# The gate table's one-hot matrices: the unscaled ones in one VectorE comparison, the scaled ones spread over three engines

## What is computed

```python
PEER_HEADS, PEER_NKEYS, PEER_TOPK = 8, 128, 16
...
best_s, best_pos = lax.top_k(cand_s.reshape(c, PEER_HEADS, -1), PEER_TOPK)
idx = jnp.take_along_axis(cand_i.reshape(c, PEER_HEADS, -1), best_pos, axis=-1)
gate = jax.nn.softmax(best_s, axis=-1)
ue = u[idx]
ve = v[idx]
act = jax.nn.gelu(jnp.einsum('td,thkd->thk', xc, ue).astype(jnp.float32), approximate=False)
return jnp.einsum('thk,thkd->td', (gate * act).astype(xc.dtype), ve)
```

## Time and profile before

| what | value |
|---|---|
| time, median of three runs | 3128.49 us |
| profiled execution, span from first to last instruction | 3124.2 us |
| what lies around the span, by the median | 4.3 us |
| PE busy | 3004.4 us, 96% |
| PEld busy | 2520.8 us, 81% |
| DVE busy | 2348.2 us, 75% |
| ACT busy | 1530.3 us, 49% |
| POOL busy | 297.5 us, 10% |
| gate stage, first layer | 1324.6 to about 1429 us |
| gate stage, second layer | 2410.3 to about 2516 us |

### The profile page before, as it was taken

The page is one execution under the profiler, slowest core; times in us unless marked ns, Lnnn a source line. Parts: engine busy times, 40 slices in busy tenths (PEclk is TensorE's granted clock), DMA queues, the critical chain, the costliest instruction groups (busy, mean ns, idle before and its releaser), DMA issues.

```text
span 3124.2 us, 51394 instructions
## 1 busy us (share of the span) xinstructions
PE 3004.4 (96%) x16392; PEld 2520.8 (81%) x16392; DVE 2348.2 (75%) x5143; ACT 1530.3 (49%) x2678; POOL 297.5 (10%) x412
## 2 busy tenths in 40 slices
PE   7999999989998999999999999999999999999998
PEld 4888887769887879877888888778798778888887
DVE  5777787556656866997777777777679977777776
ACT  3222223345754655196555554446552955555544
POOL 0000000000000005092000000000051910000000
PEclk9999999999999999999999999999999999999999
DMA  7333332223222334413555555523343135555553
GB/s 273 105 120 107 116 107 109 88 78 135 82 103 100 106 138 149 148 35 138 187 187 187 186 187 197 188 95 121 122 162 135 41 135 188 188 188 187 187 190 134
DMA packets 75386, 439.74 MB, mean 141 GB/s; under 512 B 7233, under 2 KB 8769, under 8 KB 34433
## 3 DMA queue, kind: packets, MB, share of 16 engines
q1 hardware_dynamic: 72592, 419.15, 37.8%
q0 software_dynamic: 2528, 18.02, 1.6%
q10 hardware_dynamic: 144, 0.98, 0.1%
HBM read 437.08 MB, written 1.05 MB: 140 GB/s over the span
## 4 chain that ended last, share of the span: by engine, by line
PE 84%; DVE 8%; ACT 2%; DVEq 2%; issue 2%; ACTq 0%; DMA 0%; POOL 0%; SPq 0%
PE bank L471 17%; PE bank L473 17%; PE bank L472 17%; PE bank L2341 10%; PE bank L2343 5%; PE bank L2272 4%; DVE arena L2543 2%; PE bank L1512 2%; PE bank L879 1%; PE bank L868 1%; PE bank L1229 1%; PE bank L1247 1%; PE bank L558 1%; DVE arena L1564 1%; DVEq L2543 1%
## 5 line engine op out<-in xcount | busy, mean ns | idle before, releaser
L450 ACT ACTIVATE peer_r<-wring 128x512 fp32r<-128x512 f32 x1328 | 826.5, 631 | 807.9 <-PE bank L473 538.0
L455 DVE TENSOR_TENSOR peer_r<-wring,peer_r 128x512 fp32r<-128x512 f32 x1264 | 857.5, 692 | 393.3 <-ACT peer_r L450 390.1
L2341 PE MATMUL bank<-res_r,peer_r 128*128 128x512 f32 x1344 | 479.9, 397 | 3.4 <-DVE peer_r L455 3.4
L471 PE MATMUL bank<-h_r,peer_r 128*128 128x512 f32 (+1 forms) x1088 | 397.5, 365 | 22.1 <-DVE h_r L666 15.4
L471 PE MATMUL bank<-peer_r 128*128 128x512 f32 x1024 | 404.5, 395 | 2.8 <-DVE peer_r L2574 2.8
L473 PE MATMUL bank<-peer_r 128*128 128x512 f32 x1024 | 401.3, 392 | 0.0
L472 PE MATMUL bank<-peer_r 128*128 128x512 f32 x1024 | 399.6, 390 | 0.0
L473 PE MATMUL bank<-h_r,peer_r 128*128 128x512 f32 (+1 forms) x1088 | 385.2, 354 | 0.0
L2343 PE MATMUL bank<-res_r,peer_r 128*128 128x256 f32 x1344 | 376.9, 280 | 0.0
L472 PE MATMUL bank<-h_r,peer_r 128*128 128x512 f32 (+1 forms) x960 | 334.9, 349 | 0.0
L2341 PEld LDWEIGHTS bank<-res_r,peer_r 128*128 128x128 f32 x1344 | 252.5, 188 | 64.2 <-DVE peer_r L455 4.0
(11 more groups left out here) (392 smaller groups left out, 5033.5 us busy)
## 6 DMA issues: line engine op xcount, KB each, us to landing
wring<-in_w_peer SPq DMA_DIRECT2D x256, 1024.0 KB, 4.8
wring<-in_w_proj SPq DMA_DIRECT2D x34, 1024.0 KB, 4.8
wring<-in_w_hy SPq DMA_DIRECT2D x32, 1024.0 KB, 5.3
arena<-in_w_ada POOLq DMA_DIRECT2D x16, 1024.0 KB, 5.1
wring<-in_w_out SPq DMA_DIRECT2D x16, 1024.0 KB, 4.8
wring<-in_w_ada SPq DMA_DIRECT2D x8, 1024.0 KB, 11.1
wring<-in_w_hyout SPq DMA_DIRECT2D x8, 1024.0 KB, 4.9
wring<-in_w_q SPq DMA_DIRECT2D x8, 1024.0 KB, 4.8
```

The costliest lines, as they stand in the source:

```text
L450: act.activation(SPLIT[:, buf, 0, :], raw_quarter(name, i, j, q), ACT.Copy).then_inc(split_hi, 1)
L455: v.tensor_tensor(SPLIT[:, buf, 1, :], raw_quarter(name, i, j, q), SPLIT[:, buf, 0, :].bitcast(F32), ALU.subtract).then_inc(split_lo, 1)
L471: pe.matmul(out_ap, w_hi, x_hi, start=start, stop=False, **kw)
L2341: pe.matmul(two_parts(acc[:, :]), SPLIT[:, buf, 0, w], h_both[:, k, :, :], start=(k == 0), stop=False, skip_group_check=True)
```

## The change

The unscaled one-hots of a group are now all made by VectorE, by one `tensor_tensor` comparison of 128 x 512 (the column numbers, repeated four times, against the four tokens' column, each repeated 128 times). The scaled ones are shared: GpSimd makes those of tokens 2 and 3 by `tensor_scalar` with two operations, in every group. Token 1's is made by ScalarE in three groups of four: NEAR = |iota - i|, then relu(g - g NEAR), where g is the gate weight. VectorE makes token 0's, and in the fourth case (n a multiple of 4) token 1's as well. ScalarE needs the negated gate weights for this, and two more activations ahead of the stage write them to a new array, `NEGG`. TensorE waits for `hot_c` only in the groups where ScalarE contributes.

```diff
@@
+        NEGG = wide_t[:, 2 * P:2 * P + T]
@@
                 pe.wait_ge(hot, x + 1)
                 pe.wait_ge(hot_b, x + 1)
-                pe.wait_ge(hot_c, x + 1)
+                if b:
+                    pe.wait_ge(hot_c, 3 * (x // 4) + b)
@@
             a.then_inc(pair_ready, 1)
+            for tt in range(2):
+                act.activation(NEGG[:, tt * P:(tt + 1) * P], bank[2 + tt][:, 0:P], ACT.Copy, scale=-1.0)
             act.drain()
 
             def hots_scalar(n):
 
                 act.wait_ge(g_done, GROUPS * l + n + 1)
-                t = 4 * (n % 2) + 1
-                act.activation(NEAR[:, n % 2, :], iota, ACT.Abs, scale=-1.0, bias=pair[:, 2, n // 2, t, :])
+                t, near = 4 * n + 1, NEAR[:, n % 2, :]
+                act.activation(near, iota, ACT.Abs, scale=-1.0, bias=PAIR[:, 1, t:t + 1])
                 act.drain()
-                act.activation(OHB[:, t, :], NEAR[:, n % 2, :], ACT.Relu, scale=-1.0, bias=ones[:, 0:1]).then_inc(hot_c, 1)
+                act.activation(OHA[:, t % 8, :], near, ACT.Relu, scale=NEGG[:, t:t + 1],
+                               bias=PAIR[:, 0, t:t + 1]).then_inc(hot_c, 1)
@@
-            hots_scalar(0)
             hots_scalar(1)
             for n in range(GROUPS):
-                if n + 2 < GROUPS:
+                if n + 2 < GROUPS and (n + 2) % 4:
                     hots_scalar(n + 2)
@@
-                    for s in (2, 3) if half else (0, 2, 3):
-                        a = pool.tensor_scalar(OHB[:, 4 * half + s, :], iota, pair[:, 2, i, 4 * half + s, :], None,
-                                               ALU.is_equal)
+                    for t in (4 * half + 2, 4 * half + 3):
+                        a = pool.tensor_scalar(OHA[:, t, :], iota, pair[:, 1, i, t, :], pair[:, 0, i, t, :],
+                                               ALU.is_equal, ALU.mult)
                     a.then_inc(hot_b, 1)
@@
-                t = 4 * (b % 2)
-                if b % 2:
-                    v.tensor_scalar(OHB[:, t, :], iota, pair[:, 2, 2 * i + b // 2, t, :], None, ALU.is_equal)
-                for s in range(4):
+                four = slice(4 * (b % 2), 4 * (b % 2) + 4)
+                a = v.tensor_tensor(OHB[:, four, :], wide(iota, 1, 4),
+                                    pair[:, 2, 2 * i + b // 2, four, :].to_broadcast([P, 4, P]), ALU.is_equal)
+                for s in range(1 if b else 2):
```

## The result

The changed kernel takes 3158.63 us, the median of four runs (3157.47 to 3161.14), against 3130.02 us of the kernel before on the same chip. The ratio is 1.0098, with a 95% interval of 1.0085 to 1.0112. It is slower by 29 us where 12 us of gain were forecast.

What follows compares the result with a forecast made beforehand. TensorE waits for late one-hots from VectorE, with GpSimd nearly as full, at 1.635 us a group. With a period of 1.55: 3124.2 - 10.7 - 1.2 = 3112.3 us of span, plus 4.3, said as 3117; 8-in-10 range 3106 to 3146.

Steps and rivals of the forecast that it cites:

- TensorE's floor of 1.47: Gate stage: TensorE's least time a group, 1.47 us, products 0.97 and mid step 0.50, read where groups follow with little wait.
- The rival in which TensorE becomes the bound: Gate stage: GpSimd's second operation free, collisions in idle time, period 1.47, 3106.5 us; far end of the forecast's 0.50 chance.
- VectorE's sum: Gate stage: four groups' comparisons, scaled one-hots and `gated` take 5.30 us, 1.33 a group, down from 1.6.
- ScalarE: Gate stage: ScalarE's copies and one-hots take 1.30 us a group; a relu scale from a pointer adds 0.05 at most.
- GpSimd's second operation: Gate stage, line 2459: second operation and pointer add 0.06 us an instruction, so two take 1.34 us a group.
- The high end: Line 2459: upper price of the second operation, 0.23 us from GpSimd's own rows, making two instructions 1.68 us a group.
- The collisions: Gate stage: VectorE's long comparison delays GpSimd; 0.2 us a group charged, bringing GpSimd to 1.54, the rest absorbed by idle time.
- The sum: Gate stage: GpSimd's 1.34 us plus 0.2 of collisions is 1.54 a group; period taken as 1.55, gaining 10.7 us.
- The third rival: Line 2459: GpSimd is the new, slower bound, 1.68 plus 0.15 of collisions, 1.83 us a group, 3152 us; chance 0.24.
- The fourth: Gate stage: comparison and GpSimd's pair fully exclude each other, 1.91 us a group, 33 us more, 3162 us; chance 0.06.
- The ends: Gate stage's entry: TensorE's first product waits for two GpSimd instructions, not three; gain 0.6 us a layer, 1.2 in all.
- What would show it: Signs of a wrong forecast: line 2459's median above 0.74 us, DVE's comparison above 0.8, or ACT's line 2406 waited for.

## Why the prediction was wrong

*The bound.* Right for the kernel before: TensorE waits for the one-hots, and with VectorE's load and the collisions taken off them the period falls from 1.635 to 1.53. TensorE's floor of 1.47 was read from a place that is not the tightest. The trace of the kernel before has the mid steps of two neighbouring groups only 1.32 us apart:

```profile
1325.57 0.60 PE L2290 MATMUL bank<-arena,wring 128*128 128x256 f32 x2
1326.00 1.05 PE L2304 MATMUL bank<-arena 128*128 128x128 f32 x8
1326.89 0.60 PE L2290 MATMUL bank<-arena,wring 128*128 128x256 f32 x2
```

So the floor is 1.33 us or less. The rival in which TensorE becomes the bound was priced too high by this. It didn't matter for the result, since GpSimd's term stood above both.

*VectorE's sum.* Right in its parts. The comparison lasts 0.692 us as said, the scaled one-hot 0.340 at the median. VectorE was busy 14.78 of 20 us at the longer period, 0.74 x 1.88 = 1.39 us a group against 1.33.

*ScalarE.* The relu with its scale from a pointer lasts 0.493 us where the other lasts 0.402, 0.09 more against 0 to 0.06 allowed. It did not matter.

*GpSimd's second operation.* This is the step that failed first. I took "0.06, from the row with the same difference in form", which was a row of VectorE. It measured 0.19, of which 0.114 is the operation and 0.075 the pointer. The high end, 0.23 from this engine's own price of data, was nearly right. Two instructions: 1.57 us in place of 1.34. With this and the 0.2 charged for collisions the same sum gives 1.77, a loss of 0.135 x 126 = 17 us, so beside the charged collisions this term is enough to turn the forecast gain into a loss.

*The collisions.* I charged "GpSimd 0.2 a group" and had both engines absorb the rest in idle time. They measured 2 x 0.171 = 0.34, one held instruction in each group, and nearly all of it fell on GpSimd. At 1.57 it had no idle time left to absorb them.

*The sum.* 1.57 + 0.34 = 1.91, less some overlap of neighbours, is the measured 1.87; 0.24 x 126 = 30 us. Neither step alone makes the kernel slower: with the column numbers in PSUM it takes 0.9969 of the time before, and without the second operation and pointer 0.9956. The loss needs both. The third rival (1.68 + 0.15 = 1.83 us, 3152) has the right place and nearly the right sum; it had 0.24, and my range ended at 3146, below its own price. The fourth, 3162, is nearer by its number and wrong by its mechanism: with the run's 0.785 us an instruction its rule would give 0.69 + 1.57 = 2.26 us a group, and the period is 1.87.

*The ends.* I gave 1.2 us of gain. GpSimd's first pair held TensorE from 1324.15 to 1327.04, 2.89 us where three instructions took 2.10. Both were held by a comparison: they last 1.30 and 1.33 us, and TensorE starts 0.26 behind them.

```profile
1324.15 1.30 POOL L2459 TENSOR_SCALAR arena<-const_t,arena 128x128 f32<-128x128 f32 x1 [74.22 <-ACT arena L2394]
```

It lost 0.8 in each layer.

*What would show it.* The sign named, line 2459 above 0.74 at the median, came with 0.878. Of the other, a comparison above 0.8, nothing was seen: GpSimd pays.

## What to carry to other kernels

Price an operation on the engine that will run it. If the trace has no such row there, take the high end from that engine's own rows, not the low one from a faster engine. Before giving VectorE a long instruction with two SBUF inputs beside a busy GpSimd, count GpSimd's load with the wait in it: here one GpSimd instruction for each comparison did most of its work only after the comparison's end. One operand in PSUM, if a bank is free, takes most of the wait away, and the 128 x 512 comparison was no longer for it. Idle time of an engine that absorbs a collision is to be computed after the other changes to that engine, and not before.

## What the runs showed of the hardware

- GpSimd's `tensor_scalar` of 128 x 128 in fp32 takes 0.594 us with one operation and pointer, 0.708 with a second operation and an immediate, and 0.783 with a second pointer. VectorE's goes from 0.280 to 0.340.
- A GpSimd instruction of 0.785 us that begins while VectorE's comparison with two SBUF inputs runs ends 0.58 to 0.76 us after the comparison's end (98 cases). A comparison that begins while GpSimd's instruction runs takes its usual 0.692 us at the median, 0.855 at most.
- A comparison in two halves holds GpSimd as long as the whole one, and taking instructions off GpSimd made the held ones longer, from 1.12 to 1.21 us, with one held for each comparison either way (128 and 127 for 128 comparisons).
- VectorE's one-hot with the column numbers in PSUM lasts 0.402 us at the median, and 0.340 at the median from SBUF in the changed kernel; the comparison of 128 x 512 is 0.686 and 0.692, so there the place costs nothing.
- TensorE's clock fell for a moment in the changed kernel. Behind a wait of 3.74 us for GpSimd the granted clock was 0.59 of full, so mostly at the lower of its levels of 1.2 and 2.4 GHz, and eight products' weight loads took 1.78 us where the eight before them took 0.97. Over the next 2 us it was 0.56. In the second layer the same wait was followed by full clock. From first to last mid step the first layer took 118.5 us and the second 117.6, so the lower clock can have cost about 1 us. Two windows at the entry:

```profile
1326.00:1328.00 2.00, 0.96 (x8) 0.99 (x9) 0.28 (x2) 0.00 (x0) 2.00 (x3) 1.00 0.61 231
1328.00:1330.00 2.00, 2.00 (x11) 1.80 (x10) 1.00 (x2) 1.59 (x3) 2.00 (x3) 0.59 0.03 8
```
